# Hybrid trunk kernel: the first feed-forward units interleaved, and the start and the end of attention reordered

## The chip, the cores and the metric

One core of a Trainium2 chip runs the kernel. The metric is the device time of one execution in microseconds (us), smaller is better. Engines: TensorE (PE, its weight loads PEld), VectorE (DVE), ScalarE (ACT), GpSimd (POOL) and SyncE (SP), whose queue issues nearly all DMAs.

## The reference

The input is 512 tokens of 1024 channels in float32; 16 meta tokens are put in front (528 columns in the kernel, tokens along the free axis) and dropped at the end. Two layers, each a mixer and a gated conv-FFN, each behind an RMS norm and added to the residual:

```python
h = concat([meta, x])
for i in range(2):
    hn = rms_norm(h, norm_mix_gain[i])
    if i == 0:   # S5: 64 groups of 16 channels, 64 complex states, scan over the tokens
        y = gelu(scan_output + d_skip * hn)
        val, gate = split(y @ w_glu + b_glu);  mix = val * sigmoid(gate)
    else:        # 8 heads, two score maps each, rotary q and k, causal
        a = softmax(q1 k1) - lam * softmax(q2 k2)
        mix = (rms_norm(a @ v, subln_gain) * (1 - lambda_init)) @ w_o
    h = h + mix
    hn = rms_norm(h, norm_ffn_gain[i])
    gate, val = split(causal_conv3(hn @ w_up[i]) + conv_b)
    h = h + (silu(gate) * val) @ w_down[i]      # inner width 2816
out = rms_norm(h)[16:]
```

## The kernel before

Every weight matrix is read in units of 128 columns by up to 8 k-tiles of 128 rows. SP loads unit n into `raw` (two buffers) when GpSimd has done its split of unit n - 2; ScalarE rounds it into `wH` (`split_hi`, L297), when TensorE has used the unit four before it; GpSimd writes the rest into `wL` (`split_lo`, L301). A product of float32 quality is three products: wH by xH, wH by xL, wL by xH, each over the 528 columns in two halves, so 6 matmuls for each k-tile. TensorE counts a used unit in `w_used`; the others count in `w_hi` and `w_lo`.

The activations have the same two halves. ScalarE rounds a channel tile into `hgH` (L1365), DVE writes `hgL` (L1753), and GpSimd squares the tile and adds it to `acc` (L2017, L2018). When all 8 are in, `stat_products` (L853) sums `acc` over the partitions with a matrix of ones, ScalarE takes the root (L1383), DVE the reciprocal: the norm's factor is applied after the product.

**Feed-forward.** 22 pairs of units (a gate and a value tile) go through `unit_products` (L314), then DVE's convolution, ScalarE's silu, and the down projection. Pair 0, units 0 and 1 of the stage, is done one unit after the other: its first unit waits k-tile by k-tile for hgH and hgL (`hg_ready`), then come the statistics and pair 1. Layer 0 projects down by channel tile. Layer 1 projects by token (`down_by_token`): the residual is first transposed into the eight banks of PSUM, four token tiles of two banks (L917), and all products are added to it (L927). `up_free` tells that DVE has read a pair of banks.

**Attention.** Units of w_qkv go in threes (q, k, v of a head): `unit_part(n, k0, k1)` does a part of unit n (L976). ScalarE copies the swapped halves of q and k (`rope_swap`, L1432), DVE multiplies by the cosine (`rope`, L1832), GpSimd by the sine and adds (`rope`, L2063 to L2065), between its splits. v is normed (`norm_v`, L1840), transposed by TensorE (`v_transposes`, L987) and copied (`v_out`, L1446). The 33 steps of `attend(n)` are written out on each engine: four query tiles in each of 8 heads, with one step more, 28, for the first 16 rows of all heads at once, ahead of head 7's own four (29 to 32). In step n TensorE transposes the probabilities (L1059), computes the scores of step n + 2 (`scores`, L1013, L1017), the products with v (L1083), and parts of the next head's units or of the out projection between them. DVE finds the minimum of the negated scores (`maxima`, L1845), ScalarE the exponentials (`exponentials`, L1457), DVE the difference of the two maps (`difference`, L1854 to L1856, into `Ab`) and the scaled output (`Ob`, L1882). A finished head is normed (`head_root` on ScalarE, `head_norm` on DVE, L1894, L1895), turned by TensorE (`turn_head`, L1042), and split into oH (`head_out`, ScalarE, L1499) and oL (`head_rest`, DVE, L1901). Scores of a head's last query tile reach into the bank of the turned head, and wait for its `head_rest`. After the steps `out_projection` (L1126) does the 8 units of w_o.

The order on each engine is the order in which the program is written; semaphores are all that links them. ScalarE's function tables are not managed by hand: a table load stands where the next function needs one.

Of the kernel before, what the change touches and what calls it, by code (L numbers as in the profile page):

```python
# [96 lines left out]
FREE = 1  # L97
# [43 lines left out]
def build(nc, inp, out):  # L141
# [3 lines left out]
    with ctx:  # L145
# [158 lines left out]
        def unit_products(pe, n, slot, bank, xH, xL, spans, kt0, nk, first, last, ready=None):  # L304

            pe.wait_ge(w_hi, n + 1)
            pe.wait_ge(w_lo, n + 1)
            for k in range(nk):
                kt = kt0 + k
                if ready is not None:  # L310
                    ready(kt)
                for w, x, s0, s1 in ((wH, xH, True, False), (wH, xL, False, False), (wL, xH, False, True)):
                    for b, (t0, tw) in enumerate(spans):
                        mm = nc.tensor.matmul(ps[:, bank + b, 0:tw], w[:, slot, k, :], x[:, kt, t0:t0 + tw],  # L314
                                              start=first and k == 0 and s0,
                                              stop=last and k == nk - 1 and s1)
            mm.then_inc(w_used, 1)
# [334 lines left out]
        def _(pe):  # L652
# [223 lines left out]
            def ffn(l, spans, spans_down):  # L876
                nu, nd = (U_UP0, U_DN0) if l == 0 else (U_UP1, U_DN1)

                def pair(p, q, first=False):

                    if not first:
                        pe.wait_ge(up_free[l], p + FREE)
                    for c in range(2):
                        if first and q and c:
                            pe.wait_ge(stat_sqrt[2 * l], 1)
                        unit_products(pe, p * 2 + (nu + c), 2 * q + c, 4 * (1 - q) + 2 * c, hgH, hgL, spans,
                                      0, 8, True, True, hg_ready(2 * l) if p0(p) and c == 0 else None)

                p0 = lambda p: isinstance(p, int) and p == 0
                if l == 0:  # L890
                    pe.wait_ge(glu_free, CT + FREE)
                pair(0, 0, first=True)
# [20 lines left out]
            def down_by_token():  # L913
# [27 lines left out]
                pe.wait_ge(up_free[1], FT + 1 + FREE)  # L941
                residual(0)
                residual(1)
                for kt in range(FT - 4):
                    ready(kt)
                    for t in (2, 3, 0, 1):
                        mm = products(kt, t, range(2))
                    mm.then_inc(w_used, 1)
# [183 lines left out]
            def qkv_attention():  # L1132
                unit_part(0, 0, 8)
                stat_products(1)
                unit_part(1, 0, 8)
                unit_part(2, 0, 8)
                unit_part(3, 0, 4)
                v_transposes(0)
                pe.wait_ge(mask_set, 1)
                scores(0)  # L1140
                unit_part(3, 4, 6)
                scores(1)
                unit_part(3, 6, 8)
                for n in range(NS):
                    attend(n)
# [32 lines left out]
        def _(act):  # L1178
# [282 lines left out]
            def attend(n):  # L1461
# [5 lines left out]
                if i < 2 and more:  # L1467
                    rope_swap(3 * (h + 1) + i)
                    split_next(3 * (h + 1) + i)
                if n + 2 < NS:  # L1470
# [11 lines left out]
                if i == 0 and h >= 2:  # L1482
# [21 lines left out]
            def qkv_attention():  # L1504
# [8 lines left out]
                split_next(2)  # L1513
                v_out(0)
                exponentials(0)
                exponentials(1)
                for n in range(NS):
# [22 lines left out]
        def _(dve):  # L1540
# [319 lines left out]
            def attend(n):  # L1860
# [14 lines left out]
                if n == NS - 2:  # L1875
                    head_norm(HEADS - 2)
# [3 lines left out]
                if n:  # L1880
                    dve.wait_ge(o_sq, n)
                V.tensor_scalar(Ob[:, 0 if i == NQ else h % 2, i], out_at(i), inv[:, i, 0:1], None,  # L1882
                                ALU.mult).then_inc(o_set, 1)
                if i == 1 and h and more:
                    head_norm(h - 1)
                if i == 0 and h >= 2:
# [71 lines left out]
        def _(pool):  # L1958
# [109 lines left out]
            def qkv():  # L2068
# [5 lines left out]
                for n in range(3 * HEADS):  # L2074
                    if n == 0 or n % 3 == 1:
                        rope(n)
                    split_lo(pool, U_QKV + 4 + n, n % 4)
# [35 lines left out]
```

## Time and profile before

| | us |
|---|---|
| median of 3 runs | 1291.09 (1290.28 to 1292.41) |
| the profiled execution | 1291.02 |
| its span | 1289.0 |
| TensorE busy | 1253.2 |
| DVE busy | 750.8 |
| GpSimd busy | 606.0 |
| ScalarE busy | 569.9 |

The span is measured from the first to the last instruction of the program; times in the rows count from its start. On this axis the S5 mixer takes 0 to 133, the GLU until 218, the first feed-forward until 606, attention until about 855, its out projection until 901, the second feed-forward until the end, with the down projection by token from 1156 on. TensorE's busy time counts matmuls as they overlap in its pipeline, so a busy TensorE may still run at the lower clock; the granted clock tells that.

### The profile page before, as it was taken

To read this page: it belongs to the slowest core of one execution; us is meant where nothing else is said; L and a number is where in the kernel's file an instruction comes from. 1 tells how busy PE (TensorE), PEld (TensorE's weight loads), DVE (VectorE), ACT (ScalarE), POOL (GpSimd) and SP (SyncE) were. 2 spreads that over 40 slices of the span, in tenths; PEclk is the share of its full clock that TensorE was granted. 3 is DMA by queue.
4 is the path that set the end of the run, shared out by engine and by line. 5 is a ranking of instruction groups with operands and counts; after the bars stand their busy time and mean duration, and the time that the engine had idled before them with its cause. 6 is when DMAs were issued, how large, how long until landed. Compare 5 with 4: busy or idle time off the path is not lost.

```text
span 1289.0 us, 26372 instructions
## 1 busy us (share of the span) xinstructions
PE 1253.2 (97%) x10371; PEld 1194.6 (93%) x10371; DVE 750.8 (58%) x1020; ACT 569.9 (44%) x956; POOL 606.0 (47%) x363
## 2 busy tenths in 40 slices
PE   5899999999999999999999999989999999999998
PEld 5888999999999999999889889889999999998886
DVE  8997122688888883112345555533588888882002
ACT  7996544333433432222556565633343343432113
POOL 5432666344444445656545444409644444444441
PEclk9999999999999999999999999999999999999999
DMA  8334333232233223333221122103223333233221
GB/s 172 70 69 90 91 99 98 67 93 86 81 98 98 81 78 106 92 92 115 60 66 50 52 64 63 53 17 94 88 82 98 98 92 88 80 98 98 98 98 66
DMA packets 179498, 108.88 MB, mean 84 GB/s; under 512 B 7100, under 2 KB 173789, under 8 KB 179165
## 3 DMA queue, kind: packets, MB, share of 16 engines
q1 hardware_dynamic: 178997, 107.31, 29.6%
q8 instruction: 51, 0.84, 0.3%
q10 hardware_dynamic: 432, 0.59, 0.1%
q14 instruction: 18, 0.15, 0.0%
HBM read 101.59 MB, written 2.10 MB: 80 GB/s over the span
## 4 chain that ended last, share of the span: by engine, by line
PE 36%; issue 31%; POOL 14%; DVE 13%; ACT 3%; DMA 1%; DVEq 1%; SPq 0%; POOLq 0%; ACTq 0%
PE ps L927 10%; POOL wL L301 9%; PE ps L976 9%; PE ps L817 7%; DVE cv L1791 4%; DVE cv L1797 2%; PE ps L1013 2%; PE ps L1083 1%; POOL acc L2018 1%; POOL sqt L2017 1%; DVE cg L1804 1%; DVE u L1786 1%; PE ps L314 1%; DVE u L1787 1%; ACT actH L1396 1%
## 5 line engine op out<-in xcount | busy, mean ns | idle before, releaser
L301 POOL TENSOR_TENSOR wL<-raw,wH 128x1024 fp32r<-128x1024 f32 x182 | 445.6, 2460 | 565.2 <-ACT wH L297 546.4
L297 ACT ACTIVATE wH<-raw 128x1024 fp32r<-128x1024 f32 x182 | 186.5, 1048 | 230.0 <-PE ps L314 77.0
L314 PE MATMUL ps<-hgH,wH 128*128 128x264 f32 (+1 forms) x1408 | 285.4, 284 | 1.5 <-DVE hgL L1753 1.5
L314 PE MATMUL ps<-hgH,wL 128*128 128x264 f32 (+1 forms) x1408 | 285.3, 284 | 0.0
L314 PE MATMUL ps<-hgL,wH 128*128 128x264 f32 (+1 forms) x1408 | 285.0, 284 | 0.0
L314 PEld LDWEIGHTS ps<-hgH,wH 128*128 128x128 f32 x1408 | 218.9, 189 | 2.0 <-issue 1.8
L314 PEld LDWEIGHTS ps<-hgL,wH 128*128 128x128 f32 x1408 | 218.4, 189 | 0.0
L314 PEld LDWEIGHTS ps<-hgH,wL 128*128 128x128 f32 x1408 | 217.8, 189 | 0.0
L1394 ACT ACTIVATE cg<-cg 128x528 f32<-128x528 f32 (+1 forms) x44 | 28.2, 640 | 268.1 <-DVE cg L1797 268.1
L1791 DVE TENSOR_SCALAR cv<-u,PV 128x528 f32<-128x528 f32 (+1 forms) x44 | 111.3, 2530 | 0.0
L1797 DVE SCALAR_TENSOR_TENSOR cg<-u,PV,cg 128x528 f32<-128x528 f32 (+1 forms) x88 | 97.2, 1105 | 13.0 <-DVE cv L1791 6.7
L976 PE MATMUL ps<-hgH,wH 128*128 128x264 f32 x384 | 83.6, 299 | 0.0
L976 PE MATMUL ps<-hgH,wL 128*128 128x264 f32 x384 | 78.6, 286 | 0.0
L976 PE MATMUL ps<-hgL,wH 128*128 128x264 f32 x384 | 78.4, 286 | 0.0
L314 PE MATMUL ps<-actH,wL 128*128 128x264 f32 x352 | 71.2, 283 | 0.0
L314 PE MATMUL ps<-actH,wH 128*128 128x264 f32 x352 | 71.2, 283 | 0.0
L314 PE MATMUL ps<-actL,wH 128*128 128x264 f32 x352 | 71.2, 283 | 0.0
L1797 DVE SCALAR_TENSOR_TENSOR cv<-u,PV,cv 128x528 f32<-128x528 f32 (+1 forms) x88 | 66.2, 752 | 0.0
L1457 ACT ACTIVATE Pb<-ps,tiny 128x144 f32<-128x144 f32 (+4 forms) x66 | 34.7, 531 | 69.2 <-DVE tiny L1845 69.1
L1819 DVE TENSOR_TENSOR ytok<-ps,fgain 128x512 f32<-128x512 f32 x4 | 2.8, 692 | 105.8 <-ACT ysq L1413 105.8
L976 PEld LDWEIGHTS ps<-hgH,wH 128*128 128x128 f32 x384 | 59.8, 191 | 3.9 <-issue 3.8
L1753 DVE SCALAR_TENSOR_TENSOR hgL<-hT,PV,hgH x24 | 33.6, 1401 | 46.6 <-ACT hgH L1365 46.6
(301 smaller groups left out, 2398.1 us busy)
## 6 DMA issues: line engine op xcount, KB each, us to landing
raw<-ffn_w_up SPq DMA_DIRECT2D x88, 512.0 KB, 3.8
raw<-ffn_w_down SPq DMA_DIRECT2D x38, 512.0 KB, 3.5
raw<-attn_w_qkv SPq DMA_DIRECT2D x24, 512.0 KB, 3.8
raw<-s_w_glu SPq DMA_DIRECT2D x16, 512.0 KB, 4.0
TT<-KD SPq DMA_DIRECT2D x64, 64.0 KB, 2.4
raw<-attn_w_o SPq DMA_DIRECT2D x8, 512.0 KB, 4.1
raw<-ffn_w_down SPq DMA_DIRECT2D x8, 384.0 KB, 3.4
xb<-x SPq DMA_DIRECT2D x8, 256.0 KB
```

Of the source, the lines that this page charges most:

```text
L297: nc.scalar.activation(wH[:, slot, 0:nk], raw[:, slot % 2, 0:nk], ACT.Copy).then_inc(w_hi, 1)
L301: nc.gpsimd.tensor_tensor(wL[:, slot, 0:nk], raw[:, slot % 2, 0:nk], wH[:, slot, 0:nk].bitcast(F32), ALU.subtract).then_inc(w_lo, 1)
L314: mm = nc.tensor.matmul(ps[:, bank + b, 0:tw], w[:, slot, k, :], x[:, kt, t0:t0 + tw], start=first and k == 0 and s0, stop=last and k == n ...
L817: mm = nc.tensor.matmul(ps[:, bank + b, 0:tw], w[:, n % 4, k, :], x[:, k, t0:t0 + tw], start=k == 0 and s0, stop=k == 7 and s1)
L927: mm = nc.tensor.matmul(ps[:, 2 * t + c, :], x[:, kt, tok], w[:, n % 4, 4 * c:4 * c + 4], start=False, stop=last and w is ws[-1] and x is ...
L976: mm = nc.tensor.matmul(ps[:, unit_bank(n) + b, 0:tw], w[:, n % 4, k, :], x[:, k, t0:t0 + tw], start=k == 0 and s0, stop=k == 7 and s1)
L1013: return nc.tensor.matmul(ps_row[:, base[c] + a:base[c] + b], q[half[c], q0:nk], k[half[c], a:b], start=True, stop=stop)
L1394: nc.scalar.activation(cg[:, t0:], cg[:, t0:], ACT.Silu).then_inc(silu_set[l], 1)
L1457: ins = nc.scalar.activation(Pb[:, c, 0:nk], score_row(i, c), ACT.Exp, bias=mn[:, c:c + 1], scale=-1.0, accum_out=esum[:, c:c + 1])
L1753: V.scalar_tensor_tensor(hgL[:, ds(ct, 1)], hT[:, ds(ct, 1)], PV[:, ds(gain, 1)], hgH[:, ds(ct, 1)].bitcast(F32), ALU.mult, ALU.subtract). ...
L1791: ins = V.tensor_scalar(c[k][:, t0:], u[:, k, 2 + t0:2 + L], col(i, CONV_W + (3 * l + 2) * 2 * FT + k * FT + q), col(i, CONV_B + l * 2 * F ...
L1797: ins = V.scalar_tensor_tensor(c[k][:, t0:], u[:, k, t0 + j:L + j], col(i, CONV_W + (3 * l + j) * 2 * FT + k * FT + q), c[k][:, t0:], ALU. ...
```

## The change

Seven edits: (1) the first pair of each feed-forward does k-tiles 0 to 6 of both units and then k-tile 7 of both; (2) in `down_by_token` the residual of token tiles 0 and 1 is transposed after the first products of tiles 2 and 3; (3) in attention one k-tile of the first key unit is done ahead of the statistics, and one k-tile of unit 3 fewer ahead of scores(0); (4) ScalarE gets an exponential of one column, whose result nobody reads, ahead of `v_out(0)`, and the split of unit 90 (q of head 2) goes behind the first two exponentials; (5) GpSimd rotates k of head 0 ahead of its first split; (6) GpSimd waits for the difference of step 28 before its last but one split of the stage; (7) in head 7, `head_out(5)` and `head_rest(5)` come earlier in step 29, and `head_norm(6)` after the output scaling of step 31.

```diff
 def unit_products(pe, n, slot, ..., first, last, ready=None, done=True, k0=0):
...
-                        mm = nc.tensor.matmul(ps[:, bank + b, 0:tw], w[:, slot, k, :], x[:, kt, t0:t0 + tw],
+                        mm = nc.tensor.matmul(ps[:, bank + b, 0:tw], w[:, slot, k0 + k, :], x[:, kt, t0:t0 + tw],
...
-            mm.then_inc(w_used, 1)
+            if done:
+                mm.then_inc(w_used, 1)
...
+                def first_pair():
+
+                    for k0, nk in ((0, CT - 1), (CT - 1, 1)):
+                        for c in range(2):
+                            if l == 0 and c and k0 == 0:
+                                pe.wait_ge(glu_sig, CT)
+                            last = k0 + nk == CT
+                            unit_products(pe, nu + c, c, 4 + 2 * c, hgH, hgL, spans, k0, nk, k0 == 0, last,
+                                          hg_ready(2 * l) if c == 0 else None, last, k0)
+
                 if l == 0:
                     pe.wait_ge(glu_free, CT + FREE)
-                pair(0, 0, first=True)
+                first_pair()
                 stat_products(2 * l)
...
                 residual(3)
-                pe.wait_ge(up_free[1], FT + 1 + FREE)
-                residual(0)
-                residual(1)
                 for kt in range(FT - 4):
                     ready(kt)
                     for t in (2, 3, 0, 1):
+                        if kt == 0 and t == 0:
+                            pe.wait_ge(up_free[1], FT + 1 + FREE)
+                            residual(0)
+                            residual(1)
                         mm = products(kt, t, range(2))
...
                 unit_part(0, 0, 8)
+                unit_part(1, 0, 1)
                 stat_products(1)
-                unit_part(1, 0, 8)
+                unit_part(1, 1, 8)
                 unit_part(2, 0, 8)
-                unit_part(3, 0, 4)
+                unit_part(3, 0, 3)
                 v_transposes(0)
                 pe.wait_ge(mask_set, 1)
                 scores(0)
-                unit_part(3, 4, 6)
+                unit_part(3, 3, 5)
                 scores(1)
-                unit_part(3, 6, 8)
+                unit_part(3, 5, 8)
...  ScalarE, attend(n)
+                early = i == 0 and h >= 2 and not more
+                if early:
+                    head_out(h - 2)
                 if n + 2 < NS:
                     exponentials(n + 2)
...
-                if i == 0 and h >= 2:
+                if i == 0 and h >= 2 and not early:
                     head_out(h - 2)
...  ScalarE, qkv_attention
-                split_next(2)
+                nc.scalar.activation(osq[:, 0:1], eps_col, ACT.Exp)
                 v_out(0)
                 exponentials(0)
                 exponentials(1)
+                split_next(2)
...  DVE, attend(n)
-                if n == NS - 2:
-                    head_norm(HEADS - 2)
+                early = i == 0 and h >= 2 and not more
+                if early:
+                    head_rest(h - 2)
...
                 V.tensor_scalar(Ob[:, 0 if i == NQ else h % 2, i], out_at(i), inv[:, i, 0:1], None,
                                 ALU.mult).then_inc(o_set, 1)
+                if n == NS - 2:
+                    head_norm(HEADS - 2)
...
-                if i == 0 and h >= 2:
+                if i == 0 and h >= 2 and not early:
                     head_rest(h - 2)
...  GpSimd, qkv
-                    if n == 0 or n % 3 == 1:
+                    if n == 0:
+                        rope(0)
+                        rope(1)
+                    elif n > 1 and n % 3 == 1:
                         rope(n)
+                    if n == 3 * HEADS - 2:
+                        pool.wait_ge(diff_set, FIRST_STEP + 1)
                     split_lo(pool, U_QKV + 4 + n, n % 4)
```

## Rows read from the trace of the kernel before

**Rows 1.** The page, busy time of each engine, share of the span, instructions.

```profile
PE 1253.2 (97%) x10371; PEld 1194.6 (93%) x10371; DVE 750.8 (58%) x1020; ACT 569.9 (44%) x956; POOL 606.0 (47%) x363
```

**Rows 2.** TensorE's waits: line, what for, us in total, times, longest.

```profile
PE ps L1013 <- ACT Pb L1457: 2.6, 2, 2.5
...
PE ps L314 <- DVE hgL L1753: 1.5, 2, 1.1
PE ps L1059 <- DVE Ob L1882: 1.4, 1, 1.4
PE ps L1013 <- DVE oL L1901: 1.3, 1, 1.3
PE ps L917 <- DVE u L1787: 0.9, 1, 0.9
...
PE ps L987 <- DVE u L1840: 0.8, 1, 0.8
```

**Rows 3.** Busy time by stretches of 10 us, then granted clock, DMA share, GB/s.

```profile
630.00:640.00 10.00, 7.55 (x47) 5.90 (x46) 3.26 (x9) 6.92 (x16) 3.88 (x2) 0.83 0.36 106
...
860.00:870.00 10.00, 10.00 (x73) 10.00 (x72) 1.46 (x2) 1.90 (x3) 0.41 (x1) 0.80 0.00 0
870.00:880.00 10.00, 10.00 (x73) 10.00 (x73) 6.27 (x6) 3.63 (x5) 9.68 (x6) 0.86 0.26 76
```

**Rows 4.** Timeline, 217 to 225: start, length, engine, line, tiles; idle before.

```profile
217.92 0.41 PE L314 MATMUL ps<-hgH,wH 128*128 128x264 f32 x2
...
218.65 0.41 PE L314 MATMUL ps<-hgH,wH 128*128 128x264 f32 x2
...
223.55 1.77 POOL L2018 TENSOR_TENSOR acc<-acc,sqt 128x528 f32<-128x528 f32 x1
...
224.29 0.48 PE L314 MATMUL ps<-hgH,wH 128*128 128x264 f32 x2 [1.07 <-DVE hgL L1753]
```

**Rows 5.** Timeline, 611 to 615.

```profile
611.69 1.31 POOL L2018 TENSOR_TENSOR acc<-acc,sqt 128x528 f32<-128x528 f32 x1
...
613.05 1.16 PE L853 MATMUL ps<-acc,ones 128*128 128x264 f32 x4 [0.64 <-POOL acc L2018]
```

**Rows 6.** Timeline, 628 to 660, the start of attention.

```profile
629.21 4.68 POOL L301 TENSOR_TENSOR wL<-raw,wH 128x1024 fp32r<-128x1024 f32 x2
...
630.07 1.06 ACT L297 ACTIVATE wH<-raw 128x1024 fp32r<-128x1024 f32 x1 [6.44 <-DMA raw<-attn_w_qkv]
...
631.92 1.28 ACT L1457 ACT_TABLE_LOAD   x1
...
634.10 1.27 PE L1013 MATMUL ps<-qk 64*128 64x272 f32 x4 [2.45 <-ACT Pb L1457]
...
635.46 0.79 PE L976 MATMUL ps<-hgH,wH 128*128 128x264 f32 x2
...
658.24 0.73 PE L1013 MATMUL ps<-qk 64*128 64x272 f32 x4
```

**Rows 7.** Timeline, 828 to 835, GpSimd's splits and DVE's differences.

```profile
828.71 2.38 POOL L301 TENSOR_TENSOR wL<-raw,wH 128x1024 fp32r<-128x1024 f32 x1 [3.49 <-ACT wH L297]
...
829.31 1.93 DVE L1856 SCALAR_TENSOR_TENSOR Ab<-Pb,tiny 128x128 f32<-128x128 f32 x1
...
834.54 0.37 DVE L1856 SCALAR_TENSOR_TENSOR Ab<-Pb,tiny 128x144 f32<-128x144 f32 x1
```

**Rows 8.** Timeline, 841 to 852, the last head.

```profile
841.02 0.67 ACT L1499 ACTIVATE oH<-ps,tiny 128x512 fp32r<-128x512 f32 x1
...
842.62 1.13 PE L1013 MATMUL ps<-qk 64*128 64x400 f32 x6 [1.26 <-DVE oL L1901]
...
851.47 0.35 DVE L1882 TENSOR_SCALAR Ob<-ps,tiny 128x128 f32<-128x128 f32 x1
```

**Rows 9.** Timeline, 867 to 912, out projection and what follows.

```profile
867.34 0.64 PE L1126 MATMUL ps<-oL,wH 128*128 128x264 f32 x2
...
911.22 1.33 POOL L2018 TENSOR_TENSOR acc<-acc,sqt 128x528 f32<-128x528 f32 x1
```

More of the change, by code:

```diff
@@ L302, in split_lo, with unit_products @@
                                     ALU.subtract).then_inc(w_lo, 1)
-        def unit_products(pe, n, slot, bank, xH, xL, spans, kt0, nk, first, last, ready=None):
+        def unit_products(pe, n, slot, bank, xH, xL, spans, kt0, nk, first, last, ready=None, done=True, k0=0):
             pe.wait_ge(w_hi, n + 1)
@@ L886, in pair @@
                         unit_products(pe, p * 2 + (nu + c), 2 * q + c, 4 * (1 - q) + 2 * c, hgH, hgL, spans,
-                                      0, 8, True, True, hg_ready(2 * l) if p0(p) and c == 0 else None)
-                p0 = lambda p: isinstance(p, int) and p == 0
+                                      0, 8, True, True)
+                def first_pair():
[6 more added lines that the diff above has]
+                                          hg_ready(2 * l) if c == 0 else None, last, k0)
                 if l == 0:
                     pe.wait_ge(glu_free, CT + FREE)
-                pair(0, 0, first=True)
+                first_pair()
                 stat_products(2 * l)
```

## The prediction, made before the changed kernel was run

> **What bounds the kernel now.** I read the page first: TensorE is busy 97% of the span [rows 1], so an engine's speed elsewhere matters only where TensorE stands still. Then the table of TensorE's waits [rows 2]. Past the prologue, whose first waits the change doesn't touch, the waits are few and small, about 9 us together, and nearly every one belongs to a place that the diff edits: the exponentials at the start of attention (2.6 with its echo), hgL in front of the first feed-forward units (1.5), Ob, oL and u in the last head (1.4, 1.3, 0.8), u ahead of the down projection (0.9), acc ahead of the statistics (0.6). Third, the granted clock by stretches [rows 3]: inside 630 to 640 it averages 0.83, and 0.80 and 0.86 in 860 to 880, while most stretches have full clock. The clock was at its lower level (1.2 GHz) for about 3.4 us and about 6.8 us there, the first time right after the 2.5 us standstill, the second after a run of 16-column products. So a removed wait can also give back clock.
>
> The sum is made against the profiled execution (1291.02 us, span 1289.0); the median of the runs is 1291.09, 0.07 above.
>
> **First units, first feed-forward.** One k-tile of a unit costs 218.65 - 217.92 = 0.73 us of TensorE [rows 4]. The eighth k-tile of unit 0 would have followed the pair of 222.81 after its 0.24 us, at about 223.06; it starts at 224.29, since hgL of channel tile 7 ends at 224.14. Now seven k-tiles of unit 1 (5.1 us) stand between, and the eighth of each comes at about 228.2. Gain 1.23. The new wait for the last sigmoid is free: DVE's hgL, which depends on it, ends before. The statistics come at 229.6, after acc (223.55 + 1.77 = 225.3). Nothing late is next: unit 0's weights are freed 4 us later, but ScalarE is held by the square root until the statistics anyway. Bounds 0.9 to 1.25.
>
> **Statistics in attention.** TensorE is out of unit 0 at 612.26 and waits until 613.05 for acc, which ends at 613.00 [rows 5]. One k-tile of the key unit (0.73) fills that; 0.06 stays. Gain 0.73 (bounds 0.6 and 0.8).
>
> **Start of attention.** Before, ScalarE splits a weight tile at 630.07 (waiting for its DMA), copies v, loads the exp table at 631.92 (1.28) and only then computes exp(0) from 633.21 on, to 634.05; TensorE stands from about 631.48 to 634.10, and the lower clock that follows stretches scores(1) from 0.75 (at 658.24, same shape, next product at 658.99) to 1.36 and two k-tiles from 1.47 to 2.36: 1.50 in all [rows 6]. After, on the axis of the old trace (the statistics stay at 613.05 on it): scores(0), at 629.39 before, has the 0.73 less ahead of it and one k-tile of unit 3 fewer, so it moves up by 1.47 to 627.9. It needs the rotated key. GpSimd ends the rotation of q near 624.0 as before and then spends 2.86 on that of k, which is there at 626.85; behind the split it would come at 629.2 and cost 1.3. ScalarE's own order: copy of k's halves until 621.8, split of unit 89 until 622.9, exp table until 624.4, copy of v (0.8) when it is transposed, until 628.8. DVE's maxima(0) ends 0.5 after the scores' last write, at 629.16; exp(0) takes 0.89 as before and ends at 630.1, when TensorE has just done its two k-tiles. So the wait of 2.62 falls to 0.09, and without it I take the low stretch as gone (+1.50). But something is late next. GpSimd now does both splits back to back, 626.85 to about 632.1, and DVE's Ab(0), due at 630.6, collides with them: [rows 7] show Ab(28) at 829.31 taking 1.93 where 0.37 is its time (834.54), ending 0.15 after GpSimd's split of 828.71. So Ab(0) ends at 632.2, maxima(1) at 633.0, exp(1) (1.04) at 634.1, and scores(2), which TensorE reaches at 633.4, waits 0.7. Net 2.53 + 1.50 - 0.74 = 3.3. The split of unit 90, now behind exp(1), delays the next rotation's copy by some 1.1 us; it had more slack than that at scores(3), exp(2) ending 1.3 us ahead. Bounds: 1.2 (clock stays low, stall as long as a whole split) to 4.0 (no collision).
>
> At this place the Trainium skill (SBUF — State Buffer, "SBUF: two separate sides") says that the second of two colliding instructions of DVE and GpSimd blocks fully until the first has ended. The row has it nearly so, but with only 0.15 us left to do after GpSimd's end and not 0.37. By the page's rule each collision ends 0.2 later, and the sum below would be about 7.8.
>
> **GpSimd's wait for difference(28).** It takes the split of unit 110 (2.83 at 822.40) away from Ab(27) and both splits off Ab(28). Ab(28) ends at 829.7, v is normed 1.6 earlier and the 0.96 us ahead of the v transposes goes. Behind the wait stand two splits and, through them, two loads of the out projection; their weights are first wanted at 855.27, 20 us later. But the splits now run from 829.7 to about 834.9 and hit Ab(29), due at 833.6: it ends at 835.1, where it ended at 834.91. Ob(28) and exp(30), behind it on DVE and ScalarE, come 0.2 later than before, and TensorE waits for both. So the 0.96 goes into a new wait: -0.2. Bounds -0.4 and +0.96; I take -0.2, near the low end, because the rows of the collision are the nearest there are.
>
> **Last head.** head_out(5) (0.67 at 841.02) and head_rest(5) (0.75 at 841.73) [rows 8] move ahead of exp(31) and Ob(29). TensorE has turned head 5 by 838.4 in the old trace already, so with the copies 0.67 and 0.75 behind each other oL is there at 839.9, before DVE's next instruction is due at 840.3. scores(32), at 842.62 so far, starts when TensorE is through its transposes, at 841.2: 1.4. exp(31) is held 0.06. Then Ob(31), at 851.47 behind head_norm(6) (1.06), starts when its product is there, at 849.1 with the 1.4 taken off: 0.94 more. But head_norm(6) now stands behind Ob(31) and ends at 850.6, so the turn of head 6, at 852.48 before, gains only 1.83, and oH, oL (2.0 from the turn) and with them the products at 855.27 the same. Gain 1.83, bounds 1.0 and 2.4.
>
> **First units, second feed-forward.** The gap ahead of 906.54 is 0.56. After it, the statistics would come at 912.4, but acc ends at 912.55 [rows 9]: GpSimd, back to back since 869.60, sets that. Gain 0.38, bounds 0.3 and 0.56.
>
> **Residual in the down projection.** residual(0) waited 0.9 for u [rows 2]. 12 products of 512 columns (2.8 us) now stand in front. Gain 0.88, bounds 0.7 and 0.9: one more change between transposes and products costs some 0.1.
>
> Sum: 1.23 + 0.73 + 3.3 - 0.2 + 1.83 + 0.38 + 0.88 = 8.15. 1291.02 - 8.15 = 1282.9.
>
> **Rivals.**
> - The clock stays low somewhere in 630 to 640 (the 0.7 us wait, narrow matmuls): -1.5, 1284.4. For it: the second low stretch came with hardly any idle time in front; against: TensorE has work through that stretch now. 0.18.
> - The last head gives nothing, since another member of its chain of DVE, ScalarE and TensorE takes the wait's place: 1284.7. 0.10.
> - The low stretch after 866 is shorter. Low products cost 0.44 a pair for 0.245 [rows 9], 3 us over the stretch, but the statistics at 913 wait for GpSimd, which starts at most 1.0 earlier: 1281.9. 0.09.
> - The table doesn't stay: copying v makes ScalarE load another set, and exp loads again on the path, 1.28, of which 0.9 shows: 1283.8. Against it: exp(28) to v's copy in the last head runs without a load between. The Trainium skill (ScalarE: Activation LUTs, "Table sets: the hidden batching unit") has copies in every set, which excludes this; by its 2.66 us for a switch the price would be 1.4 more. 0.05.
> - It doesn't do what it says: the small waits only move, within 2.6 us. 0.05.
> - Slower: GpSimd's new order carries into heads 1 to 6, so that a split or rotation covers Ab in most of their 24 steps. The collision of 829.31 costs TensorE 0.81 [rows 2, 7]; from 14 such steps on the kernel is slower, at 17 it takes 1282.9 + 13.8 = 1296.7. Against it: GpSimd is restarted in each head by the products of TensorE and idle in between. 0.03.
>
> **Numbers.** The forecast itself has 0.50, with 1281.8 to 1284.3 as its own range. 1281.0 to 1286.0 takes in the rivals but the last two and the pair of the first two together. A measurement can tell about 0.2% (2.6 us) from no change: faster 0.92, same 0.05, slower 0.03.
>
> **What would show it.** The hgL waits of L314 gone, both; first statistics 1.2 us earlier; the wait for Pb down from 2.5 to under 1, granted clock 1.00 around 630; a long Ab at about 630 and at 834; no wait for u ahead of the v transposes of head 7 but one for Ob or Pb soon after; the wait for oL at scores(32) gone; acc as the releaser of the third statistics. Wrong would be a total gain under 5 us, or new TensorE waits in heads 1 to 6.

## The result, and the profile after

The changed kernel takes 1282.34 us (median of 6 runs, 1281.00 to 1283.41), the kernel before, run beside it, 1292.21 (6 runs, 1290.28 to 1293.12): ratio 0.9925, 95% interval 0.9912 to 0.9937. The forecast was 1282.9. The profiled execution took 1283.41, 7.6 less than before, with a span of 1281.3; the medians are 9.9 apart. Most of the difference lies in the prologue, which the change doesn't touch: TensorE's first gated product comes 1.57 later in the profile after. The low clock of the prologue lasted 6.8 us there and 3.4 in that of before; in the fourteen profiles of this document that product starts at 118.4 to 119.3 where it lasted 3.4 and at 119.7 to 120.5 where it lasted 6.8. From there to the last matmul the gain is 9.3 us.

Busy time on the page of the changed kernel (engine, busy us, share, instructions), against [rows 1]: nothing was saved, it is all order.

```profile
PE 1252.4 (98%) x10371; PEld 1194.3 (93%) x10371; DVE 751.6 (59%) x1020; ACT 570.5 (45%) x957; POOL 606.2 (47%) x363
```

TensorE's waits in the changed kernel past the prologue (line, what for, us in total, times, longest), against [rows 2]:

```profile
PE ps L1070 <- DVE Ob L1899: 0.7, 2, 0.5
PE ps L1137 <- DVE oL L1923: 0.6, 1, 0.6
...
PE ps L1024 <- ACT Pb L1469: 0.4, 1, 0.4
PE ps L854 <- POOL acc L2037: 0.3, 1, 0.3
...
PE ps L1053 <- DVE On L1914: 0.2, 1, 0.2
```

The waits for hgL, for both u and for oL at the scores are gone, Pb fell from 2.6 to 0.4, Ob from 1.4 to 0.7; oL at the out projection rose from 0.3 to 0.6. What is left of Pb is not at the start of attention, where no wait over 0.15 is left, but in step 29, in the last head:

```profile
831.19 0.44 PE L1070 MATMUL ps<-cst,Ab 128*128 128x128 f32 x2 [0.23 <-DVE Ob L1899]
832.01 0.94 PE L1024 MATMUL ps<-qk 64*128 64x400 f32 x4 [0.38 <-ACT Pb L1469]
```

Before, the second wait for Pb (0.18, at 836.79) stood there too; it was no echo of the one at the start of attention. Stretches of 10 us of the changed kernel (busy time of TensorE, its weight loads, DVE, ScalarE and GpSimd, then the granted clock), against [rows 3]:

```profile
630.00:640.00 10.00, 9.89 (x78) 8.58 (x78) 5.48 (x11) 6.74 (x15) 5.98 (x3) 1.00 0.49 140
...
850.00:860.00 10.00, 10.00 (x83) 10.00 (x82) 1.29 (x2) 0.69 (x1) 0.00 (x0) 0.94 0.16 50
860.00:870.00 10.00, 10.00 (x62) 10.00 (x63) 4.89 (x5) 3.48 (x4) 6.26 (x4) 0.72 0.18 55
```

The clock is full where it was 0.83, and still falls for 6.8 us in the output projection. What each place gave, from the start times of the same TensorE instruction in both traces:

| from ... to (TensorE) | before | after | gain | predicted |
|---|---|---|---|---|
| first feed-forward product ... first statistics | 13.02 | 11.72 | 1.30 | 1.23 |
| statistics in attention ... Ab(4), head 1 | 52.83 | 48.32 | 4.51 | 0.73 + 3.3 |
| ... Ab(27), last step of head 6 | 161.44 | 161.13 | 0.31 | 0 |
| ... step 1 of the last head | 13.55 | 13.26 | 0.29 | -0.2 |
| ... turn of the last head | 18.17 | 16.34 | 1.83 | 1.83 |
| ... third statistics | 54.06 | 53.94 | 0.12 | 0.38 |
| residual's first transpose ... last matmul | 127.10 | 126.00 | 1.10 | 0.88 |

The stretches between these rows lose 0.16 together. The turn of the last head is its transposes in the out projection (859.04 before, 852.43 after).

The start of attention in the changed kernel (timeline: start, length, engine, line, tiles; in brackets the idle time before and who ended it), against [rows 6]:

```profile
623.26 1.28 ACT L1528 ACT_TABLE_LOAD   x1
...
629.48 0.38 ACT L1469 ACTIVATE Pb<-ps,tiny 128x144 f32<-128x144 f32 x1 [0.41 <-DVE tiny L1861]
...
633.78 1.05 ACT L297 ACTIVATE wH<-raw 128x1024 fp32r<-128x1024 f32 x1
...
627.18 4.69 POOL L301 TENSOR_TENSOR wL<-raw,wH 128x1024 fp32r<-128x1024 f32 x2
...
630.86 1.18 DVE L1872 SCALAR_TENSOR_TENSOR Ab<-Pb,tiny 128x144 f32<-128x144 f32 x1
632.08 0.72 DVE L1861 TENSOR_REDUCE tiny<-ps 128x2 f32<-128x544 f32 x1
```

exp(0) begins at 629.48, 3.7 us earlier than before (4.1 counted from the statistics), and no table load stands in front of it. Ab(0) takes 1.18 for 0.37 and ends 0.17 after GpSimd's splits.

### The profile page after: what moved, and what is told of

It reads as the page before. It is cut to its first block, busy times and chain, and to the rows that moved or that the text cites. A ratio compares the mean times of both kernels' runs of the same rounds, so it can differ in the third digit from the quotient of the medians.

```text
span 1281.3 us, 26377 instructions
## 1 busy us (share of the span) xinstructions
PE 1252.4 (98%) x10371; PEld 1194.3 (93%) x10371; DVE 751.6 (59%) x1020; ACT 570.5 (45%) x957; POOL 606.2 (47%) x363
## 4 chain that ended last, share of the span: by engine, by line
PE 86%; issue 6%; POOL 4%; DVE 2%; ACT 1%; DMA 0%; SPq 0%; POOLq 0%; DVEq 0%; ACTq 0%
PE ps L314 49%; PE ps L987 10%; PE ps L937 10%; PE ps L818 7%; PE ps L1024 2%; PE ps L1094 1%; PE ps L772 1%; POOL acc L2037 1%; PE ps L764 1%; PE ps L1070 1%; POOL sqt L2036 1%; PE ps L1028 0%; PE ps L744 0%; DVE ps L1733 0%; PE ps L711 0%
## 5 line engine op out<-in xcount | busy, mean ns | idle before, releaser
L314 PEld LDWEIGHTS ps<-hgL,wH 128*128 128x128 f32 x1408 | 218.4, 189 | 0.0
L987 PEld LDWEIGHTS ps<-hgL,wH 128*128 128x128 f32 x384 | 59.5, 188 | 0.0
```

Of the source, the lines that this page charges most:

```text
L314: mm = nc.tensor.matmul(ps[:, bank + b, 0:tw], w[:, slot, k0 + k, :], x[:, kt, t0:t0 + tw], start=first and k == 0 and s0, stop=last and k ...
L987: mm = nc.tensor.matmul(ps[:, unit_bank(n) + b, 0:tw], w[:, n % 4, k, :], x[:, k, t0:t0 + tw], start=k == 0 and s0, stop=k == 7 and s1)
```

## The experiments

The yardstick is the stretch from the statistics in attention to Ab(4), 52.83 before and 48.32 after; it leaves the prologue out. The experiments stand in the order in which they ran, each with its edit of the changed kernel. The kernel before took 1292.46 beside the first four, 1291.76 beside the next four and 1291.43 beside the last four; the ratios are to these.

**ScalarE's order put back**

```diff
-                nc.scalar.activation(osq[:, 0:1], eps_col, ACT.Exp)
+                split_next(2)
                 v_out(0)
                 exponentials(0)
                 exponentials(1)
-                split_next(2)
```

> The changed kernel with edit 4 taken back: no early exponential, the split of unit 90 again ahead of the copy of v. Stretch looked at: statistics in attention to the first transposes of head 1, 48.3 us in the changed kernel, 52.8 before. Theory (wait and clock): the table load is again on the path, TensorE stands about 2.6 to 3.3 us ahead of scores(1), the granted clock falls after it, and the stretch takes about 52, 3.5 to 4.3 more than in the changed kernel. Rival (wait only): the standstill returns, but the clock stays at its higher level, and the stretch grows by 2.6 or less. The whole kernel: 1286 by the first, 1284.5 by the second.

Measured: 1292.14, ratio 0.9998 (0.9988 to 1.0008); the stretch took 57.25, longer than in the kernel before and 5 us longer than the theory had it. One edit undone takes the whole gain of the change. ScalarE in that kernel, from the split to exp(0):

```profile
622.78 1.06 ACT L297 ACTIVATE wH<-raw 128x1024 fp32r<-128x1024 f32 x1
633.88 1.06 ACT L297 ACTIVATE wH<-raw 128x1024 fp32r<-128x1024 f32 x1 [10.04 <-DMA raw<-attn_w_qkv]
...
635.73 1.28 ACT L1469 ACT_TABLE_LOAD   x1
637.02 0.38 ACT L1469 ACTIVATE Pb<-ps,tiny 128x144 f32<-128x144 f32 x1
```

The split waits for its DMA until 633.88 (630.07 before, [rows 6]), and v's copy, the table and exp(0) wait behind it in line. The load of a weight tile needs one of raw's two buffers, and SP issues it once GpSimd has split the tile two before it (the wait for w_lo, L289). That split stands behind the key's rotation now. TensorE stands 6.8 us ahead of scores(1), and the low clock after it lasts 6.8 us instead of the 3.4 of the kernel before.

**The same, with the gap filled** by products that nobody reads

```diff
                 unit_part(3, 3, 5)
+                pe.wait_ge(rope_ps, 2)
+                for _ in range(22):
+                    nc.tensor.matmul(ps[:, 6, 0:264], wH[:, 3, 0, :], hgH[:, 0, 0:264], start=True, stop=True)
                 scores(1)
```

> As the one with edit 4 taken back, but TensorE does 22 products of 264 columns without use (2.7 us at full clock) into two free banks' first while it would stand ahead of scores(1). They compute nothing that is read. Theory (an idle TensorE is what lowers the clock, and the lower clock is a cost of its own): the granted clock stays 1.00 in 630 to 640 and the stretch from the statistics to head 1 is about 1.5 us shorter than with edit 4 taken back alone, though the useful work starts as late. Rival (the low stretch has another cause): clock and stretch as without the fill, or longer by the fill's excess.

Measured: 1292.39, ratio 1.0001 (0.9991 to 1.0010). The gap was 6.8 us and not 2.6, 4.2 of it stayed, the clock fell as without the products, for 6.8 us: it decides nothing on the clock.

**GpSimd's wait for difference(28) taken away**

```diff
-                    if n == 3 * HEADS - 2:
-                        pool.wait_ge(diff_set, FIRST_STEP + 1)
```

> The changed kernel with edit 6 taken back: GpSimd doesn't wait for the difference of step 28. Stretch looked at: transposes of step 27 to those of step 29 (8.36 us in the changed kernel, 8.92 before) and on to those of step 30 (13.26, 13.55). Theory (the gain is mostly handed on to the next wait): Ab(28) takes 1.9 again, TensorE waits 0.8 to 1.0 ahead of the v transposes, and the waits for Ob(28) and Pb after it, 0.5 to 0.8 in the changed kernel, go; up to step 30 the kernel is only 0.3 slower than the changed one. Rival (the wait's gain is kept in full): 0.95 slower up to step 30. Rival (it costs): faster by 0.2, as I had worked out.

Measured: 1282.21, ratio 0.9925 (0.9907 to 0.9943). The wait for u ahead of the v transposes is back (0.8), but at step 1 of the last head TensorE is only 0.3 later than with GpSimd's wait. Two thirds of what the edit gains at one place it gives back 5 us later.

**The wait only ahead of GpSimd's last split**

```diff
-                    if n == 3 * HEADS - 2:
-                        pool.wait_ge(diff_set, FIRST_STEP + 1)
+                    if n == 3 * HEADS - 1:
+                        pool.wait_ge(diff_set, FIRST_STEP + 2)
```

> The changed kernel with GpSimd's wait moved: the split of unit 110 goes at its old place, and only the last split (unit 111) waits, for the difference of step 29. Theory (each split that runs when DVE's difference is due holds that up until it ends, and with no split in 829 to 834 nothing waits): Ab(28) and Ab(29) both take about 0.37, neither the v transposes nor step 29's transposes nor scores(31) wait, and step 27 to step 30 takes 12.7, 0.6 less than in the changed kernel. Rival (the waits behind step 28 come from ScalarE's or DVE's own chain, not from the split): the same 13.2 to 13.3 as in the changed kernel.

Measured: 1282.82, ratio 0.9930 (0.9914 to 0.9947). Both differences, as DVE's timeline of this kernel has them, keep their own length, with GpSimd's split at 829.39 behind them:

```profile
824.67 0.35 DVE L1872 SCALAR_TENSOR_TENSOR Ab<-Pb,tiny 128x128 f32<-128x128 f32 x1
...
828.94 0.37 DVE L1872 SCALAR_TENSOR_TENSOR Ab<-Pb,tiny 128x144 f32<-128x144 f32 x1
```

From Ab(27) to step 1 of the last head it takes 12.60 (13.26 in the changed kernel). The clock stayed full in the output projection this time, so TensorE took 3.0 us less than in the changed kernel from the turn of the last head to the end of the out projection, and only 1.6 of that were left at the third statistics, where it waited 1.7 for acc. The 0.66 is plain in the trace and lost in the scatter of the runs.

**Key rotation put back behind the split**

```diff
-                    if n == 0:
-                        rope(0)
-                        rope(1)
-                    elif n > 1 and n % 3 == 1:
+                    if n == 0 or n % 3 == 1:
                         rope(n)
```

> The changed kernel with the rotation of the first key put back behind GpSimd's split; the order of ScalarE stays changed. Measured by the stretch from the statistics in attention (TensorE) to the first product with Ab of head 1: 52.8 us before, 48.3 after, 57.3 with only ScalarE's order put back. Theory (each edit has its own price): the rotated key comes 2.3 us later (one rotation is 2.86, the split 2.3 to 2.8), scores(0) waits 1.0 to 1.5 us for it, and Ab(0) no longer meets two splits in a row, so the wait for Pb falls from 0.4 to about nothing: 49.0 to 49.8 us, whole kernel 0.5 to 1.5 us slower than the changed one. Rival (the two edits are only worth something together, as the run with ScalarE's order put back suggests): the stretch goes back to about what it was before, 52 us or more, with a low clock stretch after the wait, and the kernel takes 1286 or more.

Measured: 1283.80, ratio 0.9935 (0.9916 to 0.9954); the stretch took 49.57. TensorE waits 1.4 for the rotated key and Ab(0) takes 0.37. So the rotation's place is worth 1.25 here: scores(1) comes 1.48 later without it, and 0.2 of that comes back at scores(2), since the splits no longer hold up Ab(0). The order of ScalarE works without it.

**Both edits at the start of attention put back** (the two diffs above together)

> The changed kernel with both edits at the start of attention undone: key rotation behind the split, the split of the third weight tile ahead of the copy of v, no early exponential. Same stretch (52.8 before, 48.3 after, 57.3 with only ScalarE's order put back). Theory: it was the rotation ahead of the splits that delayed the load of the third weight tile in that run; with both undone the load is early again, the wait for Pb is 2.6 to 3.4 us (one k-tile of 0.73 fewer stands ahead of it than before), the clock falls once for 3.4 us, and the stretch is 52.0 to 52.9; the kernel takes 1285.8 to 1287. Rival: that run was long for another reason (the table load behind a late copy); then this one stays above 55 us and the kernel near 1290.

Measured: 1287.61 (10 runs), ratio 0.9964 (0.9951 to 0.9977); the stretch took 53.67. The split's DMA is there at 629.38, TensorE waits 1.4 for the rotated key and 2.5 for Pb, the low clock lasts 3.4 us from 634.8 on. The theory holds for the cause; the size was 0.8 too low. At this place the kernel differs from the one before only in TensorE's own order (one k-tile ahead of the statistics, one fewer ahead of each of the first two scores), and takes 53.67 for 52.83: neither the key nor exp(0) is there earlier (scores(0) and scores(1) come 16.3 and 21.05 us after the statistics in both), so a k-tile that used to fill the wait now stands behind it. Together the two edits are worth 53.67 - 48.32 = 5.35; ScalarE's alone 53.67 - 49.57 = 4.10; the rotation's alone -3.58 (57.25). Of the 3.58, 2.87 is scores(1) coming later behind the load, and 0.71 comes after it, where the low clock lasts longer.

**The same, with the gap filled** by the 22 products

> As the run with both edits at the start of attention undone, and TensorE computes 22 products of 264 columns (0.11 us each, 2.4 us), whose result nobody reads, where it would wait for exp(0). Theory (the low clock follows the standstill): TensorE has no gap over 1 us there, the granted clock stays at 2.4 GHz through 630 to 640, and the stretch is 1.3 to 1.7 us shorter than without the products, 50.4 to 51.4. Rival (the low clock comes from the narrow products around and not from the standstill): the clock falls in the same place and the stretch stays within 0.4 us of that without the products.

Measured: 1286.79, ratio 0.9960 (0.9945 to 0.9975). TensorE without the products, and with them:

```profile
630.51 0.41 PE L987 MATMUL ps<-hgH,wL 128*128 128x264 f32 x2
633.41 0.73 PE L1024 MATMUL ps<-qk 64*128 64x272 f32 x4 [2.50 <-ACT Pb L1469]
...
635.14 0.65 PE L987 MATMUL ps<-hgH,wH 128*128 128x264 f32 x2
```

```profile
630.75 2.80 PE L1156 MATMUL ps<-hgH,wH 128*128 128x264 f32 x22
633.97 0.73 PE L1024 MATMUL ps<-qk 64*128 64x272 f32 x4 [0.41 <-ACT Pb L1472]
...
635.55 0.41 PE L987 MATMUL ps<-hgH,wH 128*128 128x264 f32 x2
```

A pair of products takes 0.41 with the gap filled and 0.65 without; the granted clock of 630 to 640 is 1.00 against 0.83. From scores(1) on to Ab(4) it takes 31.10 instead of 32.62: 1.52 us is what the low clock costs. The whole stretch is only 0.97 shorter (52.70), under what was expected, since the DMA of ScalarE's split landed 0.56 later in this profile. In these two profiles the standstill brings the clock down, not the narrow products around it; of the fourteen, the four with a wait of 2.45 us or more at the start of attention have the low clock there and the ten others do not.

**Without the early exponential**

```diff
-                nc.scalar.activation(osq[:, 0:1], eps_col, ACT.Exp)
```

> The changed kernel without the small early exponential; the split stays behind exp(1). ScalarE loads the exp table (1.28 us) after it has copied v, near 628.8 on the axis of the kernel before. Theory: exp(0) starts about 0.9 us later (the load ends 0.9 after the maxima are there), TensorE waits 1.3 us for Pb where it waits 0.4, Ab(0) comes later too, the clock does not fall: stretch 49.0 to 49.4, kernel 0.7 to 1.1 us slower than the changed one. Rival 1: the load costs nothing, since the copy of v ends early enough: 48.3. Rival 2: a wait of 1.3 us is enough to lower the clock, and 1.5 us more goes: 50.7.

Measured: 1282.80, ratio 0.9924 (0.9905 to 0.9943); the stretch took 49.00, 0.68 longer. The table is loaded at 629.39, behind v's copy, and exp(0) starts at 630.68 instead of 629.48. TensorE waits 0.8 for Pb ahead of scores(1), where it waited for nothing, and the clock stays full. With the split put back as well it was 57.25. So of the 8.93 that ScalarE's order is worth in the changed kernel, the early exponential is the small part, 0.68, and the split behind exp(1) the large one, 8.25. How the 4.10 with the key's rotation at its old place divides was not run.

**The last head's order and the statistics' place put back**

```diff
-                unit_part(1, 0, 1)
                 stat_products(1)
-                unit_part(1, 1, 8)
+                unit_part(1, 0, 8)
...
-                early = i == 0 and h >= 2 and not more
-                if early:
-                    head_out(h - 2)
...
-                early = i == 0 and h >= 2 and not more
-                if early:
-                    head_rest(h - 2)
+                if n == NS - 2:
+                    head_norm(HEADS - 2)
...
-                if n == NS - 2:
-                    head_norm(HEADS - 2)
...
```

> The changed kernel with two parts undone that lie 200 us apart, so that each shows by itself in the trace: the last head's order of copies, products and normalization as before, and the statistics in attention ahead of the first k-tile of the key unit. Theory (these two are independent of the rest): TensorE's wait for acc at the first of the statistics is 0.9 us again and the scores of the first head come 0.7 us later after it; the stretch from the first product with Ab(31) [step i1 of the last head] to the turn of the last head is 18.2 us as before (16.3 in the changed kernel); together 2.5 us, the kernel takes 1284.5 to 1285.3. Rival (as with the edits at the start of attention, the parts hang together: with the first head early, or with GpSimd's wait in place, the old order of the last head costs more or less): the last stretch differs from 18.2 us by over 0.5.

Measured: 1285.30, ratio 0.9948 (0.9933 to 0.9964). The scores of the first head come 0.71 later, and 0.50 of it is left at Ab(4). From step 1 of the last head to the turn of head 6 it is 11.60 as before (11.61; 9.70 in the changed kernel). The turn of the last head is 0.98 later still, at 19.15: the clock fell at 849.0 for 3.4 us, 1.8 us after the end of the 1.43 us wait for Ob that this order brings back. Whether the wait did it is open: in the kernel before, the same wait was not followed by a low stretch. By its number (over 0.5 from 18.2) the rival has that stretch; by the trace the order costs what it did before, and the rest is the clock.

**First pairs and residual put back**

```diff
-                first_pair()
+                for c in range(2):
+                    unit_products(pe, nu + c, c, 4 + 2 * c, hgH, hgL, spans, 0, 8, True, True,
+                                  hg_ready(2 * l) if c == 0 else None)
...
                 residual(3)
+                pe.wait_ge(up_free[1], FT + 1 + FREE)
+                residual(0)
+                residual(1)
                 for kt in range(FT - 4):
...
-                        if kt == 0 and t == 0:
-                            pe.wait_ge(up_free[1], FT + 1 + FREE)
-                            residual(0)
-                            residual(1)
```

> The changed kernel with the first pairs of both feed-forwards unit by unit again, and the residual's transposes of channel blocks 0 and 1 ahead of the products again. Theory: from the first feed-forward product to the first statistics 13.0 us as before (11.7 in the changed kernel: 1.3 lost), the same in the second feed-forward but only 0.1 to 0.4 lost since the statistics there wait for GpSimd's sum, and 0.9 to 1.1 lost between the residual's first transpose and the last matmul (127.1 us before, 126.0 in the changed one). Together 2.3 to 2.8 us: 1284.6 to 1285.2. Rival: the first unit interleaved gains less by itself, since the later units are served earlier too: under 1.5 us together, 1283.8 or less.

Measured: 1284.63, ratio 0.9953 (0.9937 to 0.9969). 13.05 to the first statistics (1.33 lost) and 127.10 from the residual on (1.10 lost), as expected. In the second feed-forward 13.07 against 12.03: 1.04 lost and not 0.1 to 0.4. TensorE stands 1.3 for hgL there and then no longer for acc, which had ended 0.55 ahead of the statistics. The low clock ahead of it also lasted only 3.4 us in this profile; from the turn of the last head it takes 53.40, where the three profiles with only edits at the start of attention or GpSimd's wait undone and the same 3.4 us take 52.6 to 52.9. So 0.5 to 0.8 is lost, still more than forecast.

**Narrow products between the wide ones**

```diff
-                wo_products(2, range(5), ALL, start=True)
-                turn_head(last)
-                wo_products(2, range(5, last), ALL)
+                for kt in range(last):
+                    wo_products(2, (kt,), ALL, start=kt == 0)
+                    if kt == 4:
+                        turn_head(last)
+                    if kt < last - 1:
+                        for n in range(2):
+                            wo_products(n, (kt,), ((0, META),))
                 for n in range(2):
                     wo_products(n, (last - 1,), ALL)
-                    wo_products(n, range(last - 1), ((0, META),))
```

> The changed kernel, but the output projection's 16-column products (the meta tokens' columns) alternate with the wide products of its unit 2 instead of following them in one run. The instructions are the same. In the profiles so far the low clock stretch after them lasted 6.8 us (four runs), 3.4 us (three) or did not come (two), with the same instructions in the same order; from the turn of the last head to the third statistics that made 53.6 to 53.9, 52.6 to 52.9, and 52.1 us. Theory (the run of narrow products brings the clock down): no low stretch there in the profile, 52.1 us or less, and the kernel is on average 0.7 to 1.5 us faster than the changed one, 1280.8 to 1281.6; no more than that, since the statistics then wait for GpSimd's sum. Rival 1: the clock falls all the same, for it follows the waits of the last head; then 52.6 to 53.9 us and 1282.3. Rival 2: more changes between weights cost as much as the clock gives back: no low stretch but 52.8 or more.

Measured: 1281.73 (5 runs), ratio 0.9921 (0.9908 to 0.9935). The stretches of 850 to 880 have the granted clock 1.00, and from the turn of head 6 to the end of the output projection (last matmul) it takes 45.42 where the changed kernel takes 48.43, 3.0 less. But the statistics wait for acc, 1.8, and after that wait the clock fell. The wait, and the stretch, in this kernel:

```profile
PE ps L854 <- POOL acc L2040: 1.8, 1, 1.8
```

```profile
900.00:910.00 10.00, 8.20 (x52) 7.73 (x51) 2.37 (x1) 3.07 (x4) 5.05 (x4) 0.83 0.27 80
```

Of the 3.0 us 1.55 is left at the statistics, and with the clock at its lower level right behind them, nothing at the residual. Full clock in the output projection here and in the next kernel does not show that the order does it, since two of the others had it with the old order.

**Both together: narrow products between, and the wait only ahead of the last split**

> The changed kernel with the narrow products alternating as in the run before this, and GpSimd's wait put ahead of its last split only, as in the run with that wait later (0.66 us gained in the last head there). Theory: both gains add up, 0.7 from the wait and 0.7 to 1.5 from the clock: 1280.2 to 1281.2, ratio about 0.991 to the kernel before. Rival: the statistics after the output projection are bound by GpSimd's sum in either case, so that the two share one gain: 1281.4 to 1282.3, no difference from the changed kernel that can be measured.

Measured: 1281.17 (5 runs, 1280.08 to 1281.63), ratio 0.9916 (0.9903 to 0.9930). The lowest median of all, at the upper end of the theory's 1280.2 to 1281.2. But its interval overlaps the changed kernel's (0.9912 to 0.9937), so it beats the kernel before and is not shown to beat the changed one. TensorE waits 1.8 for acc here too, so part of the rival stands.

## Why the prediction was right, and where it was not

**First pair.** 1.23 predicted, 1.30 measured, 1.33 in the run that undid it.

**Statistics and start of attention.** 4.03 predicted, 4.51 measured. The mechanism was as told: the table early, exp(0) off the split's DMA, key rotation first, Ab(0) hit by two splits, the clock full. Mis-sized was one term, the two splits "back to back, 626.85 to about 632.1", 5.25 us: they took 4.69, though a DVE instruction met them, and [rows 6] have two in a row at 4.68. So Ab(0) ended 0.5 earlier on the statistics' axis, scores(2) came 0.5 earlier (20.55 us after the statistics for the 21.05 of the sum), and the wait taken as 0.7 was 0.2: scores(2) starts 0.49 after the transposes in front of it, 0.31 where exp(1) is there in time. That is the whole difference. What the prediction did not see is how its parts hang together. It priced the edits as a chain in which each has its share; the runs show that the rotation's move alone costs 3.6 us, since it delays a weight load that ScalarE's old order puts ahead of exp(0), and that it gains 1.25 once the exponentials no longer stand behind that load. Nor does the k-tile ahead of the statistics have its 0.73 by itself: with the other two undone, TensorE's new order was 0.84 slower than the old one. The prediction named the delay of "the next rotation's copy" but not this one. With the other two in place, the statistics' place alone is worth 0.50 at Ab(4); the one k-tile fewer ahead of each of the first two scores was undone in no run.

**GpSimd's wait.** -0.2 predicted, +0.3 measured. It is the same term: the splits ran from 825.25 to 829.94. DVE in the changed kernel:

```profile
829.09 1.03 DVE L1872 SCALAR_TENSOR_TENSOR Ab<-Pb,tiny 128x144 f32<-128x144 f32 x1
```

It ends 0.18 after GpSimd. The structure held: the 0.96 ahead of the v transposes went, and 0.66 of it came back within two steps, as a wait for Ob (0.23) and a longer one for Pb (0.38 for 0.18), the rest in pieces too small for the table of waits.

**Last head.** 1.83 predicted and measured, 1.90 by the run that undid it, at the turn of head 6. All three edits there were priced by which instruction is due next on its engine, and each came within about 0.1 of where the prediction had it, counted from Ab(30) (oL, scores(32), Ob(31), the norm and the turn of head 6). Of the 1.90, 1.83 reach the turn of the last head. They were undone only together.

**First pair, second feed-forward.** 0.38 predicted, 0.12 measured. acc is the releaser, as forecast. Its row in the changed kernel, with the statistics behind it, against [rows 5, 9]:

```profile
904.99 1.33 POOL L2037 TENSOR_TENSOR acc<-acc,sqt 128x528 f32<-128x528 f32 x1
...
906.37 1.16 PE L854 MATMUL ps<-acc,ones 128*128 128x264 f32 x4 [0.34 <-POOL acc L2037]
```

The prediction let GpSimd's chain move with TensorE; its first split came 6.10 earlier (863.50 for 869.60) where the turn of the last head came 6.62 earlier, because more of the 6.8 us at low clock lay ahead of that split. So acc ends 53.89 us after the turn of the last head, 53.51 before. The term was also small by its own rows: statistics at 913.09 and acc's end at 912.55, with 0.05 between the two as in the rows above, leave 0.49 and not 0.38. The 0.49 less the 0.38 by which GpSimd's chain came later is about the 0.12 measured.

**Residual.** 0.88 predicted, 1.10 measured, and lost again in the run that undid it. The table's wait for u was 0.9 and is gone; the other 0.2 was not taken apart.

**Heads 1 to 6.** 0.31 gained that no step explains. In the fourteen profiles this stretch takes 161.12 to 161.17 (seven), 161.26 or 161.27 (two) or 161.43 to 161.46 (five, the kernel before among them), and no edit goes with either: 161.45 with the key rotation back, 161.13 with GpSimd's wait away. It grows from step to step by at most 0.04. It is open what sets it.

**Rivals.** Low clock in 630 to 640, the table not staying, the last head giving nothing, collisions in heads 1 to 6: none came. (Where a load does stand on the path, at 629.39 in the kernel without the early exponential, it takes 1.28 and exp(0) starts 0.01 after it: the further 1.4 of that rival's price does not show.) The shorter low stretch in the output projection did not come in the profile after but in five others (3.4 us), and in two more it was absent with the old order of the products. The statistics behind it took back part of it, as that rival said. The sum of 8.15 was 1.2 low, and the median of the kernel before was 1292.21 beside the changed one, 1.1 above the 1291.09 that the forecast began from. The two cancel in the time: that 1282.9 came so close to 1282.34 is in part luck, and closer than its steps were good for.

## What to carry to other kernels

An instruction that waits for a DMA should not stand ahead of the critical chain on an in-order engine: ScalarE's new order at one place was worth 4.1 us with the key's rotation at its old place and 8.9 with it moved, and 8.25 of the 8.9 is one weight split moved behind two exponentials. Before an edit is priced by itself, ask which other edit it relies on: undo each alone and both together, since here one part alone was worth -3.6 us and the pair +5.35. And where two engines meet at a sum, a faster one in front gains only until the other is late; look at the follower's wait in a profile in which the faster one runs well.

## What the runs showed of the hardware

**Which of two colliding instructions is stretched depends on which came first.** In the changed kernel DVE began Ab(1) 0.2 before GpSimd's split: DVE kept its 0.50 and GpSimd took 2.56 for 2.39.

```profile
634.90 2.56 POOL L301 TENSOR_TENSOR wL<-raw,wH 128x1024 fp32r<-128x1024 f32 x1 [3.03 <-ACT wH L297]
...
634.70 0.50 DVE L1872 SCALAR_TENSOR_TENSOR Ab<-Pb,tiny 128x272 f32<-128x272 f32 x1
```

With the key rotation back, GpSimd began 0.42 before DVE, and the same instruction of DVE took 2.27:

```profile
635.36 2.39 POOL L301 TENSOR_TENSOR wL<-raw,wH 128x1024 fp32r<-128x1024 f32 x1 [3.87 <-ACT wH L297]
...
635.78 2.27 DVE L1872 SCALAR_TENSOR_TENSOR Ab<-Pb,tiny 128x272 f32<-128x272 f32 x1
```

The second one does not need its whole own time behind the first: DVE ends 0.30 after GpSimd here with an own time of 0.50, and 0.15 to 0.18 after it in the three collisions of Ab(28), Ab(0) and Ab(29) above, with an own time of 0.37.

**The low clock is not the same from run to run.** The same prologue had 6.8 us of it in nine of fourteen profiles and 3.4 in five. With the products in their old order, the output projection had 6.8 us in five profiles of twelve, 3.4 in five and none in two, from the turn of the last head to the third statistics 53.6 to 54.1, 52.6 to 53.4, and 52.1 to 52.4 us. The waits of 2.45, 2.50, 4.2 and 6.8 us at the start of attention were followed by the low clock each time (four profiles). The waits of 1.3 for hgL, 1.4 for the rotated key (two profiles without a longer wait behind it) and 1.5 for acc were not. The same wait of 1.43 for Ob was in one profile and not in another, and those of 1.7 and 1.8 for acc were in one profile and not in two others. A gain under 1 us is read from stretches of a trace that leave such places out, not from the total.
